# Unmodulated RMS norms of a two-block transformer kernel: the root is applied behind the product, h is made in the residual stage, two norm vectors are folded into the weights, and the first head is loaded in pieces

## What is computed

```python
def rms_norm(x, g):
    y = xf * lax.rsqrt(jnp.mean(xf * xf, axis=-1, keepdims=True) + NORM_EPS)
    return (y * g.astype(jnp.float32)).astype(x.dtype)
...
def swiglu(h, w_gate_up, w_down):
    g, u = jnp.split(h @ w_gate_up, 2, axis=-1)
    return (jax.nn.silu(g) * u) @ w_down
...
    for l in range(DEPTH):                          # DEPTH = 2
        h = rms_norm(x, attn_norm[l])
        if l < N_A:                                 # layer 0
            x = x + diff_attention(h, ...)          # 8 heads, qkv 1024 x 3072
        else:                                       # layer 1
            kw, vw = shared_kv(x, ..., kv_norm, w_kv, k_norm)
            h = rms_norm(x, attn_norm[l])
            x = x + swa_sink_attention(h, ...)      # window 128, sinks
        x = x + swiglu(rms_norm(x, ffn_norm[l]), w_gate_up[l], w_down[l])   # hidden 2816
```

## Time and profile before

| what | value |
| --- | --- |
| median of 3 runs | 3100.03 us (3098.01 to 3102.64) |
| profiled execution | 3097.99 us, span 3096.1 us |
| mean granted TensorE clock | 0.951 |
| TensorE busy | 2809.8 us, 91% |
| VectorE busy | 1686.2 us, 54% |
| ScalarE busy | 1269.5 us, 41% |
| GpSimd busy | 639.9 us, 21% |

### The profile page before, as it was taken

How to read it: one execution, slowest core, us unless ns; L and a number is a source line. 1 busy time by engine, 2 the same in 40 slices (tenths; PEclk the granted TensorE clock), 3 DMA queues, 4 the chain that set the end, 5 groups by cost and what they waited for, 6 DMA issues and landing times.

```text
span 3096.1 us, 41620 instructions
## 1 busy us (share of the span) xinstructions
PE 2809.8 (91%) x14244; PEld 2346.1 (76%) x14244; DVE 1686.2 (54%) x2544; ACT 1269.5 (41%) x2121; POOL 639.9 (21%) x298
## 2 busy tenths in 40 slices
PE   4999899997687899997987899999997898899998
PEld 4777687886666777886876788888886787688886
DVE  5777544445665444435996464354455455464645
ACT  3444365644355364654211233132233465352422
POOL 0111087873011087873000000000000000000000
PEclk9999899998799899998997899999998999999999
DMA  3111244542100244443111111121111000222221
GB/s 121 42 44 59 82 161 168 174 156 103 41 25 18 82 169 164 170 161 104 55 49 34 55 55 61 62 68 62 60 46 46 28 28 8 69 85 92 96 94 63
DMA packets 67905, 252.07 MB, mean 81 GB/s; under 512 B 7456, under 2 KB 8736, under 8 KB 64928
## 3 DMA queue, kind: packets, MB, share of 16 engines
q1 hardware_dynamic: 67744, 249.99, 23.8%
HBM read 247.87 MB, written 2.10 MB: 81 GB/s over the span
## 4 chain that ended last, share of the span: by engine, by line
PE 44%; issue 21%; DVE 19%; POOL 7%; ACT 6%; DVEq 2%; ACTq 1%; DMA 0%; POOLq 0%
PE psum L1682 11%; PE psum L1681 11%; PE psum L1683 11%; POOL mod_p L485 7%; DVE work L1205 4%; DVE w_lo L1081 2%; DVE work L1310 1%; PE psum L2037 1%; ACT work L870 1%; PE psum L1820 1%; ACT w_hi L568 1%; DVE hx_lo L1304 1%; ACT sw_pt L882 1%; PE psum L1798 1%; PE psum L1799 1%
## 5 line engine op out<-in xcount | busy, mean ns | idle before, releaser
L1081 DVE TENSOR_TENSOR w_lo<-w_raw,w_hi 128x1024 fp32r<-128x1024 f32 (+3 forms) x334 | 451.3, 1351 | 412.6 <-ACT w_hi L568 400.3
L1681 PE MATMUL psum<-hx_hi,w_hi 128*128 128x512 f32 x1568 | 623.6, 398 | 30.0 <-DVE w_lo L1081 14.0
L1682 PE MATMUL psum<-hx_lo,w_hi 128*128 128x512 f32 x1568 | 624.8, 398 | 0.0
L1683 PE MATMUL psum<-hx_hi,w_lo 128*128 128x512 f32 x1568 | 623.3, 398 | 0.0
L485 POOL TENSOR_TENSOR mod_p<-mod_w,mod_c 128x1024 f32<-128x1024 f32 x192 | 547.7, 2884 | 186.1 <-ACT mod_p L553 150.7
L568 ACT ACTIVATE w_hi<-w_raw 128x1024 fp32r<-128x1024 f32 (+3 forms) x334 | 356.3, 1067 | 271.9 <-PE psum L1683 216.6
L475 POOL TENSOR_TENSOR tok_r<-tok_ms,half 128x4 f32<-128x4 f32 (+1 forms) x70 | 71.8, 1026 | 1857.9 <-DVE tok_ms L1005 1246.2
L1681 PEld LDWEIGHTS psum<-hx_hi,w_hi 128*128 128x128 f32 x1568 | 296.9, 189 | 81.7 <-issue 16.6
L1683 PEld LDWEIGHTS psum<-hx_hi,w_lo 128*128 128x128 f32 x1568 | 296.8, 189 | 70.3
L1682 PEld LDWEIGHTS psum<-hx_lo,w_hi 128*128 128x128 f32 x1568 | 297.4, 190 | 48.5
L1681 PE MATMUL psum<-a_hi,w_hi 128*128 128x512 f32 (+1 forms) x656 | 233.5, 356 | 18.6 <-DVE a_lo L1146 10.3
(11 more groups left out here) (263 smaller groups left out, 4972.3 us busy)
## 6 DMA issues: line engine op xcount, KB each, us to landing
mod_w<-in_w_mod SPq DMA_DIRECT2D x96, 512.0 KB, 3.6
w_raw<-in_fup SPq DMA_DIRECT2D x88, 512.0 KB, 4.5
w_raw<-in_cup SPq DMA_DIRECT2D x88, 512.0 KB, 3.5
w_raw<-in_fdown SPq DMA_DIRECT2D x32, 512.0 KB, 4.7
w_raw<-in_cdown SPq DMA_DIRECT2D x32, 512.0 KB, 3.4
w_raw<-in_da_qkv SPq DMA_DIRECT2D x8, 1536.0 KB, 6.4
w_raw<-in_fdown SPq DMA_DIRECT2D x16, 384.0 KB, 4.6
w_raw<-in_cdown SPq DMA_DIRECT2D x16, 384.0 KB, 3.0
```

Of the source, the lines that this page charges most:

```text
L1081: dve.tensor_tensor(w_lo[:, off:off + n], w_raw[:, raw:raw + n], w_hi[:, off:off + n].bitcast(F32), ALU.subtract).then_inc(s_lo, 1)
L1681: pe.matmul(dst, wh, xh, start=first, stop=False)
L1682: pe.matmul(dst, wh, xl, start=False, stop=False)
L1683: return pe.matmul(dst, wl, xh, start=False, stop=last)
```

## The change

1. **Start.** X and the first head's weights come in eight pieces each. For each k ScalarE makes `hx_hi` = X·gain and a piece of `w_hi`, VectorE `hx_lo` and `w_lo`, and TensorE multiplies them for all four token tiles, and sums the squares by matmuls with a column of ones, where VectorE did. The root scales the result when ScalarE empties PSUM. VectorE's trigonometric arithmetic goes ahead of this, and its ropes of the first tiles between the tables. ScalarE's split of head 1 goes behind four `evac_proj`.
2. **Late norms.** For both `ffn_norm` and for `kv_norm`, h without its root is made in the resid stage ahead (`feed`: ScalarE `hx_hi`, and one block later VectorE `hx_lo` and the sum of squares). TensorE starts on the next product at once and sums the squares inside it.
3. **Evacuation of the up stages.** VectorE multiplies the gate's PSUM with `root_b` (the spread root, in SBUF) and signals by a memset; ScalarE's silu reads that from SBUF; VectorE multiplies the result with `root_b` again, and then with the up tile's PSUM.
4. **Folded gains.** `kv_norm` and `attn_norm1` go into the split of the weights (`wgain`, eight pieces of 256 columns for each block), the second norm goes, and ScalarE scales by the root at evacuation.
5. **Sliding-window attention**, in both blocks: ScalarE empties a q projection at the start of an even step, where it did so at the end of an odd one, and TensorE's projection pieces stand in another order.

```diff
-    norm(gain="attn_norm0", toks=SEQ)
+    norm(toks=SEQ, late=True)
     add("heads", 8, w="da_qkv")
...
-    norm(gain="kv_norm", toks=SEQ)
-    add("kv", 2, w="sw_kv", tag="a", ctx=False)
-    norm(gain="attn_norm1", toks=SEQ, again=True)
-    add("q", 4, w="sw_q", tag="a", ctx=False)
...
+    ffn("ffn", 0, SEQ, "f", SEQ, feed="none")
+    norm(toks=SEQ, late=True)
+    add("kv", 2, w="sw_kv", tag="a", ctx=False, wgain="kv_norm")
+    add("q", 4, w="sw_q", tag="a", ctx=False, wgain="attn_norm1")
```

ScalarE, start:

```diff
+            for k in range(KT_D):
+                act.wait_ge(s_xk[k], 16)
+                act.activation(hx_hi[:, k, :], X[:, k, 0:SEQ], ACT.Copy, scale=vcol("attn_norm0", k)).then_inc(s_hhi, 1)
...
+                act.activation(w_hi[:, cols], w_raw[:, cols], ACT.Copy).then_inc(s_whi0 if k < KT_D - 1 else s_hi, 1)
+                if k >= 2:
+                    act.wait_ge(s_acc, k - 1)
+                act.activation(wk[:, k % 2, 0:SEQ], X[:, k, 0:SEQ], ACT.Square).then_inc(s_sq, 1)
```

ScalarE, linear and evac_ffn:

```diff
+                if st["kind"] == "ffn" and st.get("late"):
+                    act.wait_ge(s_rb, st["late"]["norm0"] + 1)
+                    act.activation(root_b[:], ps_lin(3, 0, SEQ), ACT.Copy).then_inc(s_rbs, 1)
...
-                        act.wait_ge(s_mm, b + (st["block0"] + 1))
-                        act.wait_ge(s_a, q + (st["tile0"] + 1))
-                        act.activation(wk[:, s // 2, 0:toks], ps_of(st, s, 0, toks), ACT.Silu).then_inc(s_gate, 1)
+                        act.wait_ge(s_gsc, q + (st["gate0"] + 1))
+                        act.activation(wk[:, s // 2, 0:toks], wk[:, s // 2, 0:toks], ACT.Silu).then_inc(s_gate, 1)
```

VectorE, residual and evac_ffn:

```diff
+                def feed(b):
+                    dve.wait_ge(s_hhi, st["feed0"] + b + 1)
...
+                    r.then_inc(s_h, 1)
+                    dve.drain()
+                    add_square(b, b)
...
+                    q = 2 * i + s // 2
+                    gate = wk[:, s // 2, 0:toks]
                     if s % 2 == 0:
+                        dve.wait_ge(s_mm, b + (st["block0"] + 1))
+                        dve.wait_ge(s_rbs, st["layer"] + 1)
+                        dve.tensor_tensor(gate, ps_of(st, s, 0, toks), root_b[:], ALU.mult).then_inc(s_ev, 1)
+                        dve.drain()
+                        dve.memset(ratio[:, 3:4], 0.0).then_inc(s_gsc, 1)
                         return
-                    q = 2 * i + s // 2
+                    dve.wait_ge(s_gate, q + (st["gate0"] + 1))
+                    dve.tensor_tensor(gate, gate, root_b[:], ALU.mult)
+                    dve.drain()
                     dve.wait_ge(s_mm, b + (st["block0"] + 1))
-                    dve.wait_ge(s_gate, q + (st["gate0"] + 1))
-                    dve.tensor_tensor(wk[:, 2 + s // 2, 0:toks], ps_of(st, s, 0, toks), wk[:, s // 2, 0:toks],
-                                      ALU.mult).then_inc(s_ev, 2)
+                    dve.tensor_tensor(wk[:, 2 + s // 2, 0:toks], ps_of(st, s, 0, toks), gate, ALU.mult).then_inc(s_ev, 1)
```

VectorE, low parts with a folded gain:

```diff
+                return dve.scalar_tensor_tensor(w_lo[:, cols], w_raw[:, raw + 256 * k:raw + 256 * (k + 1)],
+                                                vcol(st["wgain"], k), w_hi[:, cols].bitcast(F32), ALU.mult, ALU.subtract)
```

TensorE, linear:

```diff
-                pair(st, st.get("ready", 0), st["k"])
+                if st["src"] == "H" and st.get("late"):
+                    pair(st, 0, 6)
+                    sum_squares(st["late"])
+                    pair(st, 6, 8)
+                    spread_roots(st["late"])
+                else:
+                    pair(st, st.get("ready", 0), st["k"])
```

ScalarE, sliding-window attention:

```diff
-                    if p == 0:
-                        evac_proj(2)
+                    if half == 0 and m < 14:
+                        evac_proj(m + 2)
...
-                    if half and m < 13:
-                        evac_proj(m + 3)
```

More of the change, by code:

```diff
@@ L59, in make_plan @@
     stages = []
-    n = dict(block=0, lin=0, tile=0, gate=0, conv=0, norm=0, hset=0, rms=0)
+    n = dict(block=0, lin=0, tile=0, gate=0, conv=0, norm=0, hset=0, rms=0, ht=0)
     loads = [0, 0, 0, 0]
@@ L77, in add, with ffn @@
         n["conv"] += blocks if kind == "cffn" else 0
+        if kind == "resid":
+            st.setdefault("feed", None)
+            st["feed0"] = 8 * n["hset"]
         if kw.get("squares"):
             st["sq0"] = 8 * n["rms"]
+        if stages[-1]["kind"] == "norm" and stages[-1].get("late"):
+            st["late"] = stages[-1]
         stages.append(st)
     def norm(**kw):
[L83 to L85 removed]
+        stages.append(dict(kind="norm", lin0=n["lin"], norm0=n["norm"], hset0=n["hset"], rms0=n["rms"], ht0=n["ht"], **kw))
+        n["norm"] += 0 if kw.get("late") and not kw.get("spread") else 1
+        n["ht"] += 0 if kw.get("late") else 1
+        n["rms"] += 1
         n["hset"] += 0 if kw.get("final") else 1
[L88 removed]
+    def ffn(up_kind, layer, toks, tag, next_toks, gates=None, feed=None):
         t0 = groups = 0
@@ L270, in program @@
         s_constb = sem("bf16_ready")
-        s_x = sem("x_loaded")
         s_cl = sem("c_loaded")
@@ L490, in _ @@
                     modulation(st["mod"][0])
-                if st["kind"] == "norm" and not st.get("again"):
+                if st["kind"] == "norm":
                     root(0, st["toks"] // P, s_ms, st["rms0"] + 1, s_pw)
@@ L948, in swa @@
                         split(st["after"], p // 30, p // 30)
-            split(stages[1], 0, 0)
             for st in stages:
@@ L953, in _ @@
                 if k == "norm":
-                    if not st.get("final"):
+                    if not st.get("final") and not st.get("late"):
                         norm(st)
@@ L1283, in norm @@
                 toks = st["toks"]
-                if not st.get("again") and st is not stages[0]:
+                if st is not stages[0]:
                     means(st)
+                if st.get("late"):
+                    return
                 dve.wait_ge(s_rb, st["norm0"] + 1)
@@ L1434, in heads @@
                     rope_tables(da_tab_c[:, t], da_tab_s[:, t], g4, 4, t)
-                dve.drain()
+                    if t < 3:
+                        rope(t, t)
                 split(st, 1, 1)
-                for t in range(3):
-                    rope(t, t)
                 for i in range(4):
@@ L1622, in refill @@
                     cols = slice(off + D * part, off + D * (part + 1))
-                    r = dve.tensor_tensor(w_lo[:, cols], w_raw[:, raw + D * part:raw + D * (part + 1)],
-                                          w_hi[:, cols].bitcast(F32), ALU.subtract)
+                    if st.get("wgain"):
+                        for k in range(4 * part, 4 * part + 4):
+                            r = low_weights(st, off, raw, k)
+                    else:
+                        r = dve.tensor_tensor(w_lo[:, cols], w_raw[:, raw + D * part:raw + D * (part + 1)],
+                                              w_hi[:, cols].bitcast(F32), ALU.subtract)
                     if part:
@@ L1934, in kv @@
                         .then_inc(S["kpj"], 1)
+                    if n == 0 and st.get("late"):
+                        sum_squares(st["late"])
                     if 2 <= n <= nt:
@@ L2085, in _ @@
                 if k == "norm":
-                    norm(st)
+                    if not st.get("late"):
+                        norm(st)
                     hset[0] += 0 if st.get("final") else 1
```

267 lines of the change are left out of this document (176 added, 91 removed).

## The result

| | median, us | runs |
| --- | --- | --- |
| before | 3099.08 | 4 (3098.01 to 3102.64) |
| changed | 3198.92 | 4 (3197.01 to 3200.64) |

The ratio is 1.032, with a 95% interval of 1.0305 to 1.0335. The forecast was 3222 in 3125 to 3245: the sign and the mechanism hold, and the sum was 23 us too high. The profiled execution spans 3197.3 us, 101.2 more than before.

The account below looks back on a forecast made before the run. TensorE bound the networks before, a serial ScalarE-VectorE chain would bind the up stages after. Networks +146.2, clock +12.5, start -7.5, keys, values and queries -12.9 and -7.9, reordering -6: +124.4 on 3097.99, so 3222 us (3125 to 3245).

Parts of the forecast that it names:

- P: Period of four blocks in an up stage: 30.1 us forecast, against TensorE's 22.4.
- R: VectorE's second multiplication by the root in odd up-stage blocks; forecast held by GpSimd's product, running A + 5.62 to A + 6.31.
- A: Start of GpSimd's first product for a block in an up stage; the chain's times count from it.
- Rival 5: Up stages: ScalarE and VectorE overlap, P stays under 22.4, the kernel gets faster at 3043 us; chance 0.08.
- The rival with P = 33.4: Up stages: VectorE is held for whole GpSimd products, kernel 3281 us; chance 0.05.
- The clock: TensorE's clock drops after idles of near 10 us ahead of six down pairs: 6 × 2.1 = +12.5 us.
- the waits of 1.9 inside are taken to leave the clock full: Up stages: TensorE waits some 1.9 us for each block, assumed not to lower its clock.
- the way through the up stages: From `w_lo` of block 4: 3 P + 9.31 = 99.6 us, or 69.5 in part 2, plus 1.5 for the last `w_lo`.
- The start: Kernel start: head 1's split done at 61.5, 10.3 us earlier, less 2.8 for a longer half clock: -7.5 us.
- Keys, values and queries: Stages after the networks: -12.9 us from TensorE's waits, and -7.9 from dropping the second h, less the pieces' cost.
- both go: Keys and values: TensorE's waits for squares (8.1 us) and h (6.2) vanish, roots come 1.4 late: -12.9 us.
- The attentions' reordering: Both attentions: the evacuation moves into ScalarE's 40.9 us of waits for VectorE: -6 us, bounds -12 and +3.

Follow-up runs that it names:

- products of 64 columns: The changed kernel with GpSimd's products cut from 1024 to 64 columns, every other instruction kept: 3100.3 us in one run.
- blocks emptied first: The changed kernel with VectorE emptying each up-stage block before the `w_lo` three blocks on: 3046.2 us, ratio 0.983.
- the networks are as before: The changed kernel with both ffn norms and the emptying of the up stages as in the kernel before: 3058.4 us, ratio 0.9865.
- R ahead of `w_lo`: The changed kernel with only VectorE's second multiplication by the root moved ahead of `w_lo` in odd blocks: 3093.9 us, ratio 0.998.

## Why the prediction was right, and what was off

- **The bound and the chain: right, shown.** P was to be 30.1 us and is 29.99. R was to be held from A + 3.83 to A + 5.62 and done at A + 6.31: it is done at A + 6.30. The first down stage's pair began 121.7 us behind the network's start (123.3), the next two 115.8 and 85.7 (117.3 and 87.2); the last part's down blocks lost 4.8 beside the clock's 2.2, as said. That a held R and not R itself is the matter is shown by the products of 64 columns, and that its place decides by the run that only moves it. Rival 5's 3043 us is about what the kernel takes with the blocks emptied first (3046.2): ScalarE and VectorE do overlap, but in that order alone.
- **The rule of the Trainium skill** (SBUF — State Buffer, Who interferes with whom), that the later of the two is blocked for the whole instruction: R, issued 0.78 us behind the second product's start, ran as if it had begun at 2.74 behind it, of a recorded 2.88. The rule holds in its kind, but the length is what the rows said: a `w_lo` issued 1.95 behind a product's start took 1.49 to 1.57 us, so it was free at some 2.2 to 2.3 behind it and not at the recorded end. The rival with P = 33.4 took the recorded end for `w_lo` too and is out. (The losses that it lists, 2 × 0.6 and 2 × 1.4, add up to 4.0 and not to the 3.3 between 30.1 and 33.4; it is out either way.)
- **The clock: its size was off.** The six down pairs stand behind waits of 9.1 to 9.6 us; in the next 4.9 us five of them were granted 0.50, as forecast, and one 0.60. The down stages of 44.9 us took 1.8 to 2.7 us longer. But "the waits of 1.9 inside are taken to leave the clock full" failed: the waits are not even, the longest of a group is 3.4 us, and behind it the granted clock was 0.70 for 5 us. TensorE was busy for 24.7 of 30.0 us, 82% and not 75%. It cost nothing, since the chain and not TensorE set the pace.
- **Networks and clock together** were to cost 158.7 and cost 148.2 us. The term that was too large is the way through the up stages: each of the six was over 1.5 to 2.0 us sooner than in the sum, 9.9 us together. In the first network `w_lo` of block 4 began 0.5 to 0.6 us earlier, and from there to the last `w_lo` it took 98.4 and 98.5 us where the sum has 99.6 (68.4 for 69.5 in the last part).
- **The start**: -7.5 forecast, -7.0 measured, and partly by luck. Head 1's projection came at 59.45 (61.5), 12.4 us earlier and not 10.3, but 5.5 us of it were lost behind that and not 2.8: 2.1 in the next head, where the first 4.6 us were granted 0.50, and the rest spread over the heads, without a cause shown.
- **Keys, values and queries**: -20.8 forecast; -12.2, and -3.7 of waits for h inside the first projection, measured. The step that failed is "both go": with no norm in between, the first weights of the next stage are what is late, 6.5 us at the head and 7.8 ahead of the first q projection. The price of a block's pieces was nearly right (2.7 us, and 2.35 measured), but it is paid at both places, 4.6 us in all.
- **The attentions' reordering: wrong in size, -6 against -21.2** (11.0 without h's waits, and 10.2). The step that failed was to price the move by ScalarE's wait that it fills, and to put TensorE's part of it at nothing. Without the context over half of the gain is TensorE's busy time, at a higher granted clock, and the rest is TensorE's waits, such as those for the softmax weights (`sw_pt`). TensorE's order mattered as much as ScalarE's. Which of the waits sets the clock back is not shown.

Together: the networks 10.5 us too dear, the reordering 15.2 too little, the keys and values 4.9 too much, and the remaining stretches 2.4 too little: that makes the 23 us.

What stays open: whether ScalarE's scaling and pieces are what makes the old orders slower in the changed kernel than in that of before, where 4.7 us in the attention and its output projection go when the networks are as before, and why the granted clock in the keys and values differs between executions.

## What to carry to other kernels

Ask of an added instruction not how long it takes but what stands behind it in its queue, and who waits for that: two engines that had been busy for 39% and 62% of a group became the bound, because in every block each had to wait for the other's last instruction. Empty what is done ahead of preparing what is three blocks away; with that order in the up and the down stages the same instructions gain 2.1% where they had lost 3.2%. And price a reordering by the waits of the engine that bounds the kernel, in both orders together: half of a matched pair of orders can be worse than none.

## What was not expected of the hardware

A held VectorE instruction shows the hold as its own duration (2.65 us for 0.69 of work), and no wait stands in the profile, so a part of VectorE's busy share beside GpSimd's products is no work. GpSimd's side grows too: where VectorE's instructions with two SBUF operands stood closer together, six products took 18.08 us instead of 17.3. And TensorE's clock fell to its lower level not only behind waits of 9 us: behind one of 3.4 us the next 5 us were granted 0.70 on average, while behind one of 2.0 us (blocks emptied first), and in a stretch with a wait of 0.9 (R ahead of `w_lo`), the granted clock was 1.00.
